# Two-block transformer on one core: pooling as running sums on GpSimd, mixers between the steps of attention, turns two steps later

## The chip, the cores and the metric

The kernel runs as one program on one core of a Trainium2 chip. Its time is the device time of one execution in microseconds (us). Before the change three runs gave 1590.38, 1590.78 and 1592.57 us; the median is 1590.78. TensorE does matmuls and transposes, VectorE (DVE), ScalarE (ACT) and GpSimd (POOL) elementwise work; each engine works through its own instructions in order and waits on semaphores. SyncE (SP) issues the loads of weights, in order too.

## The reference, cut to what matters

The model is a first block of two layers over an image stream x (256 tokens) and a context stream (256 tokens), then a second block with routed experts. All is in float32, width 1024. In each layer of the first block, three mixers read slices of one projection, and one output projection reads their results:

```python
zx = hx @ w_in[i]                      # 1280 columns: q 512, k 128, v 128, pool 256, fourier 256
mx = concatenate([
    latent_attention(q, k, v, kc, vc), # 8 heads of 64; keys: 256 context + 256 image
    pool_mix(zx[..., KV_END:POOL_END], w_pool[i], pool_scale[i]),
    fourier_mix(zx[..., POOL_END:], w_four[i]),
], axis=-1)
x = x + ga1 * (mx @ w_out[i])
if update_ctx:                         # layer 0 only: the same for the context stream
    mc = concatenate([context_attention(qc, kc, vc), pool_mix(...), fourier_mix(...)], axis=-1)

def pool_mix(u, w_pool, pool_scale):   # four groups of 64 channels, windows 2, 4, 8, 16
    means = (cs[hi] - cs[lo]) / cnt    # mean over tokens t-w/2 .. t+w/2-1, cut at the ends
    d = means - u
    return einsum('blgc,gcd->blgd', d, w_pool) * pool_scale

def fourier_mix(u, w_four):            # four groups of 64 channels
    f = fft2(u, axes=(tokens, channels), norm='ortho').real
    return einsum('blgc,gcd->blgd', f, w_four)
```

A SwiGLU follows in each layer, and then the second block, whose 32 experts of 6 MB each are the bulk of the 392 MB read from HBM.

## The kernel before, in words

Activations are held transposed: channels on partitions, tokens along the free axis, the streams side by side (512 columns in layer 0, 256 in layer 1). Each linear layer runs over tiles of 128 output channels (pe_tile, L1056 to L1074). Weights and activations are split into a high and a low part (WH, WL; HH, HL; GH, GL), and a tile is three products: high times high and high times low (L1067, L1068), then low times high (L1073). ScalarE makes the high part of a weight tile (act_split, L1026) and VectorE the low part (dve_split, L1036).

pe_layer runs, on TensorE, the in-projection of ten tiles, attention, the mixers, the output projection (eight tiles), then SwiGLU. Between the in-projection's tiles stand small jobs (pe_in_mid, pe_in_end): head norms, rotary turns, the transposes of rows (pe_rows, L1184; copy L1190), and "fills", products with the modulation weights w_ada (pe_ada, L672), which may run anywhere before they are needed. Five of ten tiles are transposed by rows: v (row 0), two pooling and two Fourier tiles (rows 1 to 4).

Attention runs in steps. A step is 128 queries of a pair of heads, g = 0 and 1. Group (0, 1) of layer 0 has 8 steps against 512 keys ("large" below) and 8 of the context stream against 256 keys ("small"); layer 1 has 8 large ones. In step x TensorE does the scores of step x into banks 0 and 1 (pe_scores, L1391), the values of the pair of steps x-3, x-2 if x is odd (pe_values, L1448), and the turns of step x-1, which are the transposes of the probabilities (pe_turn, L1422). VectorE takes the maximum (L1396) and divides (L1409, L1411), ScalarE exponentiates (L1403) and copies the turned probabilities out (act_turned, L1430). pe_scores waits until the exponentials of the step before have read the two banks (s_ex). Results are copied to MU by VectorE (L1641), from there to GH by ScalarE (L1655), and the low part is made by VectorE (L1647).

The mixers come when attention has ended (pe_mixers). Pooling is a product with a 256 by 256 matrix per window, from the table k_pool (L1695), then with w_pool (L1712). Fourier is a product along the tokens (L1701), one along the channels (L1709, L1710) and one with w_four (L1712), with copies by ScalarE between them (L1719).

SyncE fills a ring of ten slots of 1 MB. A load is issued when its slot's former content has been used. The tables k_pool and k_mix hold a slot each until the mixers have ended (consts, load.used). After the output projection TensorE waits for the norm; the fills of GAP stand there.

## Time and profile before

| what | value |
|---|---|
| median of three runs | 1590.78 us |
| the profiled execution | 1592.6 us, its span 1590.8 us |
| TensorE busy | 1392.6 us (88% of the span) |
| VectorE, ScalarE, GpSimd busy | 709.6, 522.5, 39.2 us |
| mean granted TensorE clock | 0.941 of full speed |
| layer 0: attention, mixers | 120.94 to 175.6, 175.6 to 195.0 us |
| layer 1: attention, mixers | 682.1 to 717.8, 717.8 to 731.8 us |
| transfers | 394.51 MB, mean 248 GB/s |

A busy TensorE is not TensorE at its peak, since matmuls are pipelined and a record begins while its weights or its neighbour still run. In the chain of what ended last TensorE has 65%, transfers 23%, VectorE 5% and ScalarE 4%.

### The profile page before, as it was taken

To read this page: it belongs to the slowest core of one execution; us is meant where nothing else is said; L and a number is where in the kernel's file an instruction comes from. 1 tells how busy PE (TensorE), PEld (TensorE's weight loads), DVE (VectorE), ACT (ScalarE), POOL (GpSimd) and SP (SyncE) were. 2 spreads that over 40 slices of the span, in tenths; PEclk is the share of its full clock that TensorE was granted. 3 is DMA by queue.
4 is the path that set the end of the run, shared out by engine and by line. 5 is a ranking of instruction groups with operands and counts; after the bars stand their busy time and mean duration, and the time that the engine had idled before them with its cause. 6 is when DMAs were issued, how large, how long until landed. Compare 5 with 4: busy or idle time off the path is not lost.

```text
span 1590.8 us, 24639 instructions
## 1 busy us (share of the span) xinstructions
PE 1392.6 (88%) x10297; PEld 1043.4 (66%) x10297; DVE 709.6 (45%) x1296; ACT 522.5 (33%) x967; POOL 39.2 (2%) x40
## 2 busy tenths in 40 slices
PE   6998899999999999989999999998896676676664
PEld 3664587887878787747899998898653333333332
DVE  4336546675655444664655657576421101101101
ACT  4425524222222223554543445465320110110001
POOL 1000020000000010001000000000000000000000
PEclk9999999999999999999999999999797877887878
DMA  8983043635845343705756449245799999999996
GB/s 340 412 278 122 1 159 115 219 129 183 321 161 168 114 155 106 221 16 223 234 170 211 134 172 306 89 133 219 289 420 424 426 426 426 426 426 426 426 426 266
DMA packets 160221, 394.51 MB, mean 248 GB/s; under 512 B 11605, under 2 KB 124777, under 8 KB 126058
## 3 DMA queue, kind: packets, MB, share of 16 engines
q1 hardware_dynamic: 159530, 391.44, 65.1%
q8 instruction: 84, 1.38, 0.3%
q10 hardware_dynamic: 576, 1.44, 0.2%
q14 instruction: 31, 0.25, 0.0%
HBM read 391.80 MB, written 1.05 MB: 247 GB/s over the span
## 4 chain that ended last, share of the span: by engine, by line
PE 65%; DMA 23%; DVE 5%; ACT 4%; issue 2%; SPq 0%; DVEq 0%; ACTq 0%
DMA R<-in_w_dram 22%; PE ps L1067 15%; PE ps L1073 14%; PE ps L1068 14%; PE ps L2965 3%; PE ps L1095 2%; PE ps L1089 2%; PE ps L1090 2%; PE ps L672 2%; DMA R<-in_w_ada_dram 1%; PE ps L1448 1%; PE ps L1391 1%; PE ps L3015 1%; PE ps L3044 1%; PE ps L1701 1%
## 5 line engine op out<-in xcount | busy, mean ns | idle before, releaser
L1036 DVE TENSOR_TENSOR WL<-R,WH 128x1024 fp32r<-128x1024 f32 (+1 forms) x201 | 224.5, 1133 | 162.8 <-ACT WH L1026 162.8
L2965 PE MATMUL ps<-R,XG 128*32 128x256 f32 x2048 | 176.0, 505 | 117.9 <-DMA R<-in_w_dram 112.3
L1067 PE MATMUL ps<-HH,WH 128*128 128x256 f32 (+2 forms) x872 | 273.6, 336 | 0.3 <-ACT WH L1026 0.3
L1068 PE MATMUL ps<-HL,WH 128*128 128x256 f32 (+2 forms) x872 | 270.0, 330 | 0.0
L1026 ACT ACTIVATE WH<-R 128x1024 fp32r<-128x1024 f32 (+1 forms) x201 | 190.1, 961 | 138.8 <-PE ps L1073 109.4
L2965 PEld LDWEIGHTS ps<-R,XG 128*32 128x32 f32 x2048 | 86.8, 139 | 201.8 <-issue 186.9
L1067 PEld LDWEIGHTS ps<-HH,WH 128*128 128x128 f32 (+1 forms) x872 | 164.2, 188 | 25.1 <-issue 8.1
L1068 PEld LDWEIGHTS ps<-HL,WH 128*128 128x128 f32 (+1 forms) x872 | 164.9, 189 | 16.5
L1073 PE MATMUL ps<-HH,WL 128*128 128x256 f32 (+2 forms) x872 | 164.6, 330 | 0.0
L1067 PE MATMUL ps<-GH,WH 128*128 128x512 f32 (+1 forms) x480 | 153.9, 339 | 0.0
L1068 PE MATMUL ps<-GL,WH 128*128 128x512 f32 (+1 forms) x480 | 153.4, 339 | 0.0
L1073 PEld LDWEIGHTS ps<-HH,WL 128*128 128x128 f32 (+1 forms) x872 | 133.6, 187 | 17.9 <-issue 1.1
L3004 DVE TENSOR_TENSOR HT<-ps,SIL 128x128 f32<-128x128 f32 x32 | 9.3, 292 | 297.9 <-ACT SIL L2998 297.9
L2974 ACT ACTIVATE U<-ps 128x256 f32<-128x256 f32 x32 | 19.8, 619 | 337.8 <-PE ps L2965 337.8
L1067 PEld LDWEIGHTS ps<-GH,WH 128*128 128x128 f32 x480 | 90.3, 188 | 11.8 <-issue 0.8
L1068 PEld LDWEIGHTS ps<-GL,WH 128*128 128x128 f32 x480 | 90.2, 188 | 10.9
L1073 PE MATMUL ps<-GH,WL 128*128 128x512 f32 (+1 forms) x480 | 93.3, 340 | 0.0
L1073 PEld LDWEIGHTS ps<-GH,WL 128*128 128x128 f32 x480 | 75.6, 188 | 11.0
L1147 DVE SCALAR_TENSOR_TENSOR XT<-ps,MOD,XT 128x256 f32<-128x256 f32 x80 | 36.4, 480 | 91.0 <-PE ps L1073 90.9
L1747 ACT ACTIVATE GH<-TMP 128x512 fp32r<-128x512 f32 (+1 forms) x44 | 23.1, 525 | 138.8 <-DVE TMP L1757 138.8
L3015 PE MATMUL ps<-R,HT 128*32 128x256 f32 x1024 | 62.5, 382 | 5.9 <-DVE HT L3004 3.1
L694 DVE SCALAR_TENSOR_TENSOR R<-R,SC,R 128x2048 f32<-128x2048 f32 x28 | 65.1, 2346 | 0.0
(494 smaller groups left out, 1733.9 us busy)
## 6 DMA issues: line engine op xcount, KB each, us to landing
R<-in_w_dram SPq DMA_DIRECT2D x192, 1024.0 KB, 26.5
R<-in_w_ada_dram SPq DMA_DIRECT2D x72, 1024.0 KB, 7.8
R<-in_w_gate_up_dram SPq DMA_DIRECT2D x40, 1024.0 KB, 6.9
R<-in_w_in_dram SPq DMA_DIRECT2D x20, 1024.0 KB, 9.3
R<-in_w_down_dram SPq DMA_DIRECT2D x16, 768.0 KB, 4.4
R<-in_w_down_dram SPq DMA_DIRECT2D x16, 640.0 KB, 4.3
R<-in_w_in_dram SPq DMA_DIRECT2D x8, 512.0 KB, 7.4
R<-in_w_out_dram SPq DMA_DIRECT2D x16, 256.0 KB, 8.5
```

The source lines that it names most:

```text
L672: last = e.matmul(PS[6][32 * g:32 * g + 32, :], SC[:, k, :], R[load.slot][:, 512 * g:512 * g + 512], start=(k == 0), stop=(k == 7))
L694: e.scalar_tensor_tensor(sums[x][:, :], R[load.slot][:, :], SC[:, k, v:v + 1], sums[x][:, :], ALU.mult, ALU.add)\
L1026: last = e.activation(H, w, ACT.Copy)
L1036: last = e.tensor_tensor(L, w, H.bitcast(F32), ALU.subtract)
L1067: e.matmul(b[0:n, 0:N], H[:, k, 0:n], xh(k, N), start=(k == 0), stop=False)
L1068: e.matmul(b[0:n, 0:N], H[:, k, 0:n], xl(k, N), start=False, stop=False)
L1073: last = e.matmul(b[0:n, 0:N], L[:, k, 0:n], xh(k, N), start=False, stop=(k == K - 1))
L1089: e.matmul(b[:, 0:N], room[t0 + j][0][:, k, :], xh(k, N), start=(k == 0), stop=False)
L1090: e.matmul(b[:, 0:N], room[t0 + j][0][:, k, :], xl(k, N), start=False, stop=False)
L1147: e.scalar_tensor_tensor(XT[:, j, sl], bank_of(t)[:, sl], MOD[:, i, gate + j, col:col + 1], XT[:, j, sl], ALU.mult, ALU.add).then_inc(s_xr, 1)
L2965: mm = e.matmul(PS[4][32 * g:32 * g + 32, 0:256], x[:, 4 * hf + k, :], w[g // 2][:, k, 256 * (g % 2):256 * (g % 2) + 256], start=(hf == 0 ...
L3015: mm = e.matmul(PS[6][32 * g:32 * g + 32, 0:256], HT[b % 2][:, 2 * hf + k, :], w[:, k, 256 * g:256 * g + 256], start=(hf == 0 and k == 0), ...
```

## The change

Pooling no longer uses a matrix. The in-projection's pooling tiles are copied into ZP, with 8 zero columns around each stream, and GpSimd adds shifted copies of them: windows of 2, 4, 8 and 16 come from one another, then a product with 1/count and a subtraction, 12 operations for both tiles (pool_windows). TensorE keeps the product with w_pool. For Fourier, the channel matrices are first multiplied with w_four (pe_four_weights, copied to FW), the tiles are multiplied by FW instead of transposed (pe_four_rows, copied to ZF), and one product along the tokens is left. k_pool goes.

The mixers stand between attention's steps: MIX_AT gives for a layer the step x at which one is issued, "p" pooling (tile), "f" Fourier (stream, tile), in bank 7. Scores alternate between banks 0, 1 and 5, 6; there are six probability buffers instead of four; turns are those of step x-2, values come one step later. ScalarE and VectorE make GH and GL from PSUM directly (act_high, dve_low), without MU. Both first output tiles are split during attention, and pe_out_first runs seven of eight blocks of each around the last values. Two fills go from layer 0's attention to the gap after its output projection, two from layer 1's attention into its in-projection.

```diff
-K_POOL, K_DFT, K_R1, K_D, K_RD, K_CD, K_SD = 0, 0, 1024, 1152, 1408, 1664, 1792
+K_DFT, K_R1, K_IC, K_CD, K_SD = 0, 1024, 1152, 1664, 1792
 K_END = 1920
+WINDOWS = (2, 4, 8, 16)
...
+        (oH + 18 * KB, oH + 20 * KB, oH + 22 * KB, oH + 8 * KB, oH + 10 * KB, oH + 12 * KB))]
...
-        consts.append((const_load("k_pool", 2048), const_load("k_mix", K_END)))
+        consts.append(const_load("k_mix", K_END))
...
-        plan_ada(2)
-        for load in consts[i]:
-            load.used = (s_mx, 30 if i else 20)
+        if i:
+            plan_ada(2)
+        consts[i].used = (s_mx, MIXED[i])
...
-                    plan_ada(4 if i else 6)
+                    plan_ada(4 if i else 8)
...
+    def pe_out_first(e, i, xh, xl, ready):
+        t, early, late = first_of["out", i], (4, 5, 0, 1, 6, 2, 7), (3,)
+        pe_begin(e, t)
+        pe_high(e, t, xh, xl, early, ready)
+        pe_values(e, *pair_at(i, len(STEPS[i]) + 2))
+        pe_begin(e, t + 1)
+        pe_high(e, t + 1, xh, xl, early, None)
+        for j in range(2):
+            pe_high(e, t + j, xh, xl, late, ready, begins=False)
+            pe_low(e, t + j, xh, 8)
...
+    def pe_four_weights(e, i):
+        kc = R[consts[i].slot]
+        e.wait_ge(d_ring[consts[i].slot], consts[i].landed)
+        e.wait_ge(d_wp, 128 * (i + 1))
+        e.wait_ge(s_z, i + 1)
+        e.wait_ge(s_mod, 7 if i else 2)
+        for j in range(2):
+            for x, c in enumerate((K_CD, K_SD)):
+                last = e.matmul(PS[7][:, 256 * j + 128 * x:256 * j + 128 * x + 128], kc[:, c:c + 128], WPF[:, 2 + j, :], start=True,
+                                stop=True)
+        last.then_inc(s_fm, 1)
...
+    def pe_four_rows(e, i, j, r):
+        n = round_at(i, j, r)
+        e.wait_ge(s_evi, 10 * i + 9 + j)
+        e.wait_ge(s_zf, n)
+        if (j, r) == (1, 0):
+            e.wait_ge(s_mod, TURNS.index(MORE_TURNS[i]) + 1)
+        for a in range(2):
+            c = 128 * (2 * r + a)
+            last = e.matmul(PS[7][:, 256 * a:256 * a + 256], ZT[1 + j][:, c:c + 128], FW[:, j, :], start=True, stop=True)
+        last.then_inc(s_fm, 1)
+    def dve_four_rows(e, i, j, r):
+        n = round_at(i, j, r)
+        e.wait_ge(s_fm, n + 1)
+        e.tensor_copy(ZF[:, 2 * r:2 * r + 2, j, :], PS[7][:, :].rearrange("p (a n) -> p a n", a=2)).then_inc(s_zf, 1)
...
+    WINDOW_OPS = 12
+    def pool_windows(e, i):
+        n = STREAMS_IN[i]
...
+        e.wait_ge(s_mm, first_of["in", i] + 4)
...
+        e.wait_ge(d_ring[consts[i].slot], consts[i].landed)
+        e.wait_ge(s_pads, PADS[i])
+        e.wait_ge(s_evi, 10 * i + 7)
+        e.tensor_tensor(A[:, 1:W], x0[:, 0:W - 1], x0[:, 1:W], ALU.add).then_inc(s_pm, 1)
+        e.wait_ge(s_pm, done + 1)
+        e.tensor_tensor(B[hi, 2:W - 1], A[hi, 1:W - 2], A[hi, 3:W], ALU.add).then_inc(s_pm, 1)
...
+        e.wait_ge(s_evi, 10 * i + 8)
+        e.tensor_tensor(B[:, 1:W], x1[:, 0:W - 1], x1[:, 1:W], ALU.add).then_inc(s_pm, 1)
+        e.wait_ge(s_pm, done + 6)
+        e.tensor_tensor(A[:, 2:W - 1], B[:, 1:W - 2], B[:, 3:W], ALU.add).then_inc(s_pm, 1)
...
+        e.wait_ge(s_pm, done + 11)
+        e.tensor_tensor(streams_in(x1, n), streams_in(B, n), streams_in(x1, n), ALU.subtract).then_inc(s_pm, 1)
...
-        return () if i else FILLS.get(j, ())
+        return {8: (38,), 9: (39,)}.get(j, ()) if i else FILLS.get(j, ())
...
+    def score_bank(v, g):
+        return PS[(0, 1, 5, 6)[2 * (v // 2 % 2) + g]]
...
-        if s or A == 1:
-            e.wait_ge(s_ex, 16 * A + 2 * s)
-        else:
+        if x >= 2:
+            e.wait_ge(s_ex, v - 2)
+        elif x == 0:
             e.wait_ge(*bank_out(i, 0))
             e.wait_ge(*bank_out(i, 1))
+        else:
+            e.wait_ge(s_rope, 15 * i + 15)
+            e.wait_ge(s_at, TURNS.index(MORE_TURNS[i]) + 1)
...
+        if v >= 6:
+            e.wait_ge(s_tn, v - 5)
+        e.activation(P1[v % 6][:, 0:n], score_bank(v, g)[:, 0:n], ACT.Exp, bias=stats(v)[:, 0:1], accum_out=stats(v)[:, 1:2])\
+            .then_inc(s_ex, 1)
...
-    def fills_at(A, s):
-        return {(0, 1): (24,), (0, 3): (25,), (2, 0): (38,), (2, 1): (39,)}.get((A, s), ())
...
+    MIX_AT = [{5: ("p", 0), 7: ("p", 1), 9: ("f", 0, 0), 11: ("f", 1, 0), 13: ("f", 0, 1), 14: ("f", 1, 1)},
+              {3: ("p", 0), 5: ("p", 1), 7: ("f", 0, 0), 8: ("f", 0, 1)}]
...
+        t = x - 3
+        if t < 1 or t % 2 == 0 or t >= len(STEPS[i]):
             return None
-        A, s = steps[x - 2]
+        A, s = STEPS[i][t]
...
+    def pe_mix(e, i, op):
+        kc, o = R[consts[i].slot], MIX[i].index(op)
+        if o == 0:
+            e.wait_ge(s_zf, FIRST_COPY[i] + 1 + len(ROUNDS[i]))
+        else:
+            e.wait_ge(s_gl, mix_out(i, MIX[i][o - 1]) + 1)
+        if op[0] == "p":
+            j = op[1]
+            e.wait_ge(s_pm, WINDOW_OPS * i + (5, 12)[j])
+            for s in range(STREAMS_IN[i]):
+                last = e.matmul(PS[7][:, 256 * s:256 * s + 256], WPF[:, j, :], ZP[j][:, 264 * s + 8:264 * s + 264], start=True, stop=True)
+        else:
+            _, s, j = op
+            for t in range(2):
+                for x in range(2):
+                    c = K_DFT + 512 * t + 256 * x
+                    last = e.matmul(PS[7][:, 0:256], ZF[:, 2 * s + t, j, 128 * x:128 * x + 128], kc[:, c:c + 256],
+                                    start=(t == 0 and x == 0), stop=(t == 1 and x == 1))
+        last.then_inc(s_mx, 1)
...
+    def act_high(e, op):
+        o, (m, cols) = OUTS.index(op), out_place(op)
+        if op[1] == "pair":
+            e.wait_ge(s_pv, 8 * op[2] + 2 * op[3] + 2)
+        else:
+            e.wait_ge(s_mx, mixed_by(op))
+        if op[1] == "p":
+            e.activation(GH[:, m, cols], out_bank(op), ACT.Copy, scale=out_scale(op)).then_inc(s_gh, 1)
+        else:
+            e.activation(GH[:, m, cols], out_bank(op), ACT.Copy).then_inc(s_gh, 1)
...
+    def dve_low(e, op):
+        o, (m, cols) = OUTS.index(op), out_place(op)
+        e.wait_ge(s_gh, o + 1)
+        high = GH[:, m, cols].bitcast(F32)
+        if op[1] == "p":
+            e.scalar_tensor_tensor(GL[:, m, cols], out_bank(op), out_scale(op), high, ALU.mult, ALU.subtract).then_inc(s_gl, 1)
+        else:
+            e.tensor_tensor(GL[:, m, cols], out_bank(op), high, ALU.subtract).then_inc(s_gl, 1)
...
+    def pe_attention(e, i):
+        steps = STEPS[i]
+        n = len(steps)
+        for x in range(n + 2):
+            if x < n:
                 pe_scores(e, *steps[x])
+            if x == 0:
+                pe_ada_turn(e, MORE_TURNS[i])
+            for j, r in four_round_at(i, x):
+                pe_four_rows(e, i, j, r)
+            if pair_at(i, x):
+                pe_values(e, *pair_at(i, x))
+            if x in MIX_AT[i]:
+                pe_mix(e, i, MIX_AT[i][x])
+            if x >= 2:
+                pe_turn(e, *steps[x - 2])
+    SPLIT_AT = ((12, 13), (7, 9))
+    def act_attention(e, i):
+        steps = STEPS[i]
+        n = len(steps)
+        for x in range(n + 4):
+            for op in outs_at(i, x - 1):
+                act_high(e, op)
             for g in range(2):
+                if x < n:
                     act_exp(e, *steps[x], g)
             for g in range(2):
+                if 2 <= x < n + 2:
+                    act_turned(e, *steps[x - 2], g)
+            if x in SPLIT_AT[i]:
+                act_split(e, first_of["out", i] + SPLIT_AT[i].index(x))
+    def dve_attention(e, i):
+        steps = STEPS[i]
+        n = len(steps)
+        for x in range(n + 4):
+            for g in range(2):
+                if x < n:
+                    dve_max(e, *steps[x], g)
+            if x == 0:
+                dve_ada(e, MORE_TURNS[i])
+            for j, r in four_round_at(i, x):
+                dve_four_rows(e, i, j, r)
+            if 1 <= x <= n:
                 for g in range(2):
+                    dve_divide(e, *steps[x - 1], g)
+            for op in outs_at(i, x - 1):
+                dve_low(e, op)
+            if x - 1 in SPLIT_AT[i]:
+                dve_split(e, first_of["out", i] + SPLIT_AT[i].index(x - 1))
...
-    GAP = {1: tuple(range(26, 32)), 2: tuple(range(32, 38)), 3: tuple(range(40, 44)), 4: tuple(range(44, 48))}
+    GAP = {1: tuple(range(24, 32)), 2: tuple(range(32, 38)), 3: tuple(range(40, 44)), 4: tuple(range(44, 48))}
...
-        pe_attention(e, (2,) if i else (0, 1))
-        pe_mixers(e, i)
+        pe_attention(e, i)
+        pe_out_first(e, i, gh, gl, waiting(e, mixed(i)))
...
+            pool_windows(e, 0)
             pool_sum_columns(e)
             pool_sums(e, 1, 512)
             pool_sums(e, 2, 512)
+            pool_windows(e, 1)
...
```

TensorE, step 11 of layer 0 (small), before: KTr,QT are scores, RES,P turns, PT,Z values; numbers behind names are buffers.

```order
L1391 MATMUL ps<-KTr,QT 128x256 [waits s_ex]
L1391 MATMUL ps<-KTr,QT 128x256
L1448 MATMUL ps<-PT_115,Z 64x256 [waits s_ot,s_z,s_pt]
L1448 MATMUL ps<-PT_116,Z 64x256
L1448 MATMUL ps<-PT_115,Z 64x256
L1448 MATMUL ps<-PT_116,Z 64x256
L1422 MATMUL ps<-RES,P_110 128x128 [waits s_pt,s_nrm]
L1422 MATMUL ps<-RES,P_110 128x128
L1422 MATMUL ps<-RES,P_111 128x128 [waits s_pt,s_nrm]
L1422 MATMUL ps<-RES,P_111 128x128
```

The same engine in the changed kernel, from the scores of step 11 (R,ZF is the Fourier mix):

```order
L1517 MATMUL ps<-KTr,QT 128x256 [waits s_ex]
L1517 MATMUL ps<-KTr,QT 128x256
L1636 MATMUL ps<-R_63,ZF 128x256 [waits s_gl]
L1636 MATMUL ps<-R_63,ZF 128x256 x3
L1549 MATMUL ps<-RES,P_113 128x128 [waits s_pt,s_nrm]
L1549 MATMUL ps<-RES,P_113 128x128
L1549 MATMUL ps<-RES,P_114 128x128 [waits s_pt,s_nrm]
L1549 MATMUL ps<-RES,P_114 128x128
L1517 MATMUL ps<-KTr,QT 128x256 [waits s_ex]
L1517 MATMUL ps<-KTr,QT 128x256
L1572 MATMUL ps<-PT_119,Z 64x256 [waits s_gl,s_z,s_pt]
L1572 MATMUL ps<-PT_120,Z 64x256
```

A mix stands between the scores and the turns, the turned probabilities are those of two steps before, and the mix waits on s_gl, VectorE's low part of the mix before it.

VectorE, step 5 of layer 0, before (ps is PSUM, P the probabilities):

```order
L1396 TENSOR_REDUCE ST<-ps 128x1 [waits s_sco] x2
L1641 COPY MU_108<-ps 128x256 [waits s_pv]
L1409 RECIPROCAL ST<-ST 128x1 [waits s_ex]
L1411 TENSOR_SCALAR P_112<-P_112,ST 128x512 [waits s_rcp]
L1409 RECIPROCAL ST<-ST 128x1 [waits s_ex]
L1411 TENSOR_SCALAR P_113<-P_113,ST 128x512 [waits s_rcp]
```

VectorE in the changed kernel, the same step (L1663 is the low part of values, straight from PSUM):

```order
L1522 TENSOR_REDUCE ST<-ps 128x1 [waits s_sco] x2
L1536 RECIPROCAL ST<-ST 128x1 [waits s_ex]
L1538 TENSOR_SCALAR P_115<-P_115,ST 128x512 [waits s_rcp]
L1536 RECIPROCAL ST<-ST 128x1 [waits s_ex]
L1538 TENSOR_SCALAR P_116<-P_116,ST 128x512 [waits s_rcp]
L1663 TENSOR_TENSOR GL<-ps,GH 128x256 [waits s_gh]
```

The divides (P) are now those of the step before the maximum's, and the copy to MU is gone.

GpSimd in the changed kernel, layer 0's running sums for the second pooling tile; before, this engine had nothing there:

```order
L1294 TENSOR_TENSOR ZS_76<-ZP_74 128x535 [waits s_evi]
L1296 TENSOR_TENSOR ZS_75<-ZS_76 128x533 [waits s_pm]
L1298 TENSOR_TENSOR ZS_76<-ZS_75 128x529 [waits s_pm]
L1300 TENSOR_TENSOR ZS_75<-ZS_76 64x521 [waits s_pm]
L1301 TENSOR_TENSOR ZS_76<-ZS_76,R_63 64x2x256
L1303 TENSOR_TENSOR ZS_76<-ZS_75,R_63 64x2x256 [waits s_pm]
L1305 TENSOR_TENSOR ZP_74<-ZS_76,ZP_74 128x2x256 [waits s_pm]
```

Each waits for the one before it (s_pm); the first waits for ScalarE's copy of the tile (s_evi).

## Rows read from the trace of the kernel before

**Rows 1.** The page's 40 slices: share of the transfer engines in tenths.

```profile
DMA  8983043635845343705756449245799999999996
```

**Rows 2.** Stretches: us, busy PE PEld DVE ACT POOL, clock, transfers.

```profile
121.00:153.30 32.30, 25.99 (x159) 13.18 (x158) 21.98 (x54) 18.90 (x48) 0.00 (x0) 0.95 0.42 139
153.30:175.60 22.30, 17.72 (x122) 9.77 (x124) 16.84 (x60) 16.10 (x57) 0.00 (x0) 1.00 0.01 1
175.60:195.00 19.40, 18.71 (x81) 11.08 (x79) 7.48 (x16) 9.09 (x21) 0.00 (x0) 1.00 0.00 1
682.10:717.80 35.70, 29.05 (x184) 15.09 (x185) 22.72 (x56) 21.34 (x52) 0.00 (x0) 0.95 0.00 0
717.80:731.80 14.00, 10.35 (x43) 5.39 (x40) 4.73 (x10) 5.34 (x11) 0.00 (x0) 1.00 0.01 1
```

**Rows 3.** Timeline, large steps: start us, us, engine, line, what, [idle before].

```profile
141.89 1.13 PE L1391 MATMUL ps<-KTr,QT 64*128 64x512 f32 x4 [1.42 <-ACT P L1403]
...
145.85 1.13 PE L1391 MATMUL ps<-KTr,QT 64*128 64x512 f32 x4
...
147.01 1.29 DVE L1396 TENSOR_REDUCE ST<-ps 128x1 f32<-128x512 f32 x2 [0.43 <-PE ps L1391]
147.74 0.69 ACT L1403 ACTIVATE P<-ps,ST 128x512 f32<-128x512 f32 x1 [0.83 <-DVE ST L1396]
...
149.08 1.08 ACT L1430 ACTIVATE PT<-ps 128x512 f32<-128x512 f32 x2
...
149.24 1.13 PE L1391 MATMUL ps<-KTr,QT 64*128 64x512 f32 x4 [1.23 <-ACT P L1403]
...
150.30 1.95 PE L1448 MATMUL ps<-PT,Z 128*64 128x256 f32 x16
...
152.18 1.09 PE L1422 MATMUL ps<-RES,P 128*128 128x128 f32 x8
```

**Rows 4.** Chain of waits, small steps: start us, us, what.

```profile
161.24 0.70 PE ps L1391 x4
161.95 1.06 PE ps L1448 x8
...
165.82 0.70 PE ps L1391 x4
```

**Rows 5.** Chain of waits, layer 1's mixers.

```profile
725.19 0.45 PE ps L1710 x2
...
726.86 1.73 PE ps L1701 x4
```

**Rows 6.** Timeline of the gap after layer 0's output projection.

```profile
243.70 4.50 PE L672 MATMUL ps<-R,SC 128*32 128x512 f32 x40
...
247.18 0.89 DVE L926 SCALAR_TENSOR_TENSOR HL<-TMP,MOD,HH 128x256 fp32r<-128x256 f32 x2 [0.18 <-ACT HH L876]
```

**Rows 7.** GpSimd's additions by line: shortest, median, longest in ns.

```profile
L818 POOL TENSOR_TENSOR TMP<-TMP,TMP x20: 737/1301/2207, 208.0 to 945.9; 128x512 f32<-128x512 f32 x10, 128x256 f32<-128x256 f32 x10
```

**Rows 8.** Timeline: GpSimd's additions and VectorE's splits beside them.

```profile
207.85 1.22 DVE L1036 TENSOR_TENSOR WL<-R,WH 128x1024 fp32r<-128x1024 f32 x1
208.02 2.20 POOL L818 TENSOR_TENSOR TMP<-TMP,TMP 128x512 f32<-128x512 f32 x1 [12.47 <-DVE TMP L805]
...
213.55 1.30 POOL L818 TENSOR_TENSOR TMP<-TMP,TMP 128x512 f32<-128x512 f32 x1 [3.33 <-ACT TMP L798]
214.46 1.47 DVE L1036 TENSOR_TENSOR WL<-R,WH 128x1024 fp32r<-128x1024 f32 x1 [1.65 <-ACT WH L1026]
```

**Rows 9.** The page's loads: what, issuer, KB, median us to landing.

```profile
R<-in_w_gate_up_dram SPq DMA_DIRECT2D x40, 1024.0 KB, 6.9
```

**Rows 10.** Timeline of SyncE from the first expert load.

```profile
1053.28 141.72 SPq L2611 DMA_DIRECT2D R<-in_w_dram  x48
```

**Rows 11.** Timeline, end of the in-projections of layer 0 and layer 1.

```profile
108.49 1.99 PE L1270 MATMUL ps<-QT,R 128*128 128x256 f32 x8 [1.44 <-DVE QT L1257]
...
681.13 0.42 DVE L1190 COPY Z<-ps 128x256 f32<-128x256 f32 x1
```

More of the change, by code:

```diff
@@ L553, in block_program @@
         j = t - first_of["in2"]
-        tile.bank = t % 4 if j < 0 else j if j < 4 else (j - 4) % 3 if j < N_IN2 else (j - N_IN2) % 4
+        out = next((t - first_of["out", i] for i in range(2) if 0 <= t - first_of["out", i] < 8), None)
+        tile.bank = out % 4 if out is not None else t % 4 if j < 0 else j if j < 4 else (j - 4) % 3 if j < N_IN2 else (j - N_IN2) % 4
         tile.after = last_in.get(tile.bank)
@@ L1051, in block_program, with pe_begin @@
     bank_free = {}
-    def pe_tile(e, t, xh, xl, ready, mid=None):
-        tile, b = tiles[t], bank_of(t)
-        n, N = tile.n, tile.N
-        H, L = room[t][0:2]
-        K = sum(p[2] for p in tile.parts)
+    def pe_begin(e, t):
+        tile = tiles[t]
         if t in bank_free:
@@ L1482, in act_attention, with outs_at, attention_out, mix_out @@
-    def act_attention(e, group):
-        steps = steps_of(group)
-        for x in range(len(steps) + 2):
+    def outs_at(i, x):
+        mix, pair = MIX_AT[i].get(x), pair_at(i, x)
+        return ([(i, *mix)] if mix else []) + ([(i, "pair", *pair)] if pair else [])
+    OUTS_OF = [[op for x in range(len(STEPS[i]) + 3) for op in outs_at(i, x)] for i in range(2)]
+    OUTS = OUTS_OF[0] + OUTS_OF[1]
+    def attention_out(A, m):
+        return OUTS.index((A_LAYER[A], "pair", A, m))
+    def mix_out(i, op):
+        return OUTS.index((i, *op))
@@ L1660, in block_program @@
[L1660 to L1672 removed]
     for i in range(2):
+        end = (32, 48)[i]
         for j in range(4):
[L1676 to L1678 removed]
@@ L1714, in act_mixers @@
[L1714 to L1733 removed]
+            bank_free[first_of["out", i] + j] = (s_ex, end - 2) if j < 2 else (s_pt, end)
@@ L1875, in act_layer @@
         t1 = first_of["gu", i, 0]
-        act_linear(e, first_of["out", i], 8, sums(2 * i + 1, ("out", i)), begun=1, then=t1)
+        act_linear(e, first_of["out", i], 8, sums(2 * i + 1, ("out", i)), begun=2, then=t1)
         act_split(e, t1 + 1)
```

392 lines of the change are left out of this document (160 added, 232 removed).

## The prediction

> **What bounds the kernel now.** I read the page's 40 slices first: the DMA row says that only the last quarter of the span is bound by transfers [rows 1]. That tail can't start by itself: its loads go out from 1053 us on, when ring slots come free behind the second block's compute [rows 10], so a microsecond saved in the first block moves the whole tail forward by one. Then I read the stretches around the change [rows 2]. In layer 0 attention takes 32.3 + 22.3 us (image queries against 512 keys, then context queries against 256) and the mixers after it 19.4 us, until the output projection starts: 74.0 us. In layer 1 it is 35.7 + 14.0 = 49.7 us. In none is TensorE full: 26.0 of 32.3, 17.7 of 22.3, 29.1 of 35.7. In the mixers' stretches VectorE and ScalarE idle more than half the time.
>
> Last, the pace of attention, step by step. Two large steps take 7.35 us (scores at 141.89 and at 149.24) [rows 3], two small ones 4.58 us (161.24, 165.82) [rows 4]. What sets 7.35: scores to their first reduce 1.16, to the first exponential 0.73, two exponentials 1.34, two copies of turned probabilities 1.08, hand-over 0.1, and on TensorE values 1.88 and turns 1.02.
>
> **Does attention itself get faster?** It has one more pair of score banks, six probability buffers and turns two steps late, so scores no longer wait for the exponentials of the step just before. But ScalarE's order in a step is exponentials of step x, then the turned copies of step x-2, and the values of a pair, on TensorE in the step after, wait for those copies. Call S the moment at which TensorE starts the scores of an odd step. The exponentials are done at S + 1.16 + 0.73 + 1.34 = 3.23, the copies of the second half of the pair at 4.31, values start at 4.4, end at 6.3, turns follow to 7.3, and only then come the next odd scores. That is 7.3 us for two steps [rows 3], as now. So I give attention no faster pace. What the order buys is the hole between S + 3 (scores, turns, next scores issued) and S + 4.4: a mixer's matmuls fit there.
>
> **Layer 0, summed from the first scores to the output projection.**
> - Start, to the scores of step 5: first scores, a turn of the ada block, two Fourier rounds whose copies (0.7 each, near a reduce of that width, 1.29 for two) are queued on VectorE ahead of the first two divides, no overlap yet: 15.4 us by following the queue with the durations of [rows 3].
> - Steps 5 to 8, two pairs, with both pooling mixes (two matmuls of 256 columns, 0.45 each [rows 5]) in the hole: 2 x 7.3 = 14.6.
> - Steps 9 and 10 are small, with a Fourier mix of four 256-column matmuls, priced as the two of 512 columns now, 1.73 [rows 5]. TensorE sets it: 0.7 scores + 1.73 + 1.02 turns of a large step + 0.65 for their copy on ScalarE + 0.1, then the last large values 1.88 and small turns 0.5: 6.6.
> - Steps 11 and 12: 0.7 + 1.73 + 0.5 + 0.7, values 1.06 [rows 4], turns 0.5: 5.2.
> - Steps 13 and 14 hold a mix each in one bank. The second waits for VectorE's low half of the first, and VectorE has the first output tile's split (1.22, as the split in [rows 8]) and the maxima and divides of two steps ahead of it. Behind it on TensorE wait the turns of step 12 and the scores of step 15: 8.9 for the pair.
> - Steps 15 to 17, draining: 5.0. Then the projection begins, with the last values (1.06) inside: seven of eight blocks of tile 0 cover the copy that they wait for.
> Sum 15.4 + 14.6 + 6.6 + 5.2 + 8.9 + 5.0 + 1.1 = 56.8 against 74.0: 17.2 less. This pays for itself mostly by the mixers' 19.4 us lying beside attention.
>
> **Layer 1.** Same start but one Fourier round: 14.6 to step 5; steps 5 and 6 7.3; from step 7 with a Fourier mix in steps 7 and 8, the second waiting for the low half of the first: values end at 6.4, low half at 6.4, mix to 8.2, turns of step 6 to 9.2, their copy, turns of step 7 to 10.4; last values in the projection 1.9. Sum 34.2 against 49.7: 15.5 less.
>
> **In-projection, both layers.** Four row transposes with copies go; a product of the Fourier matrices (four matmuls of 128 columns, one copy) and two rounds (one in layer 1) come. In layer 0 a copy ahead of the last head products goes, where TensorE idles 1.44 us [rows 11], but TensorE gets about 0.7 more afterwards: +0.4. In layer 1 the last row copy before the scores goes (681.13 [rows 11]), and two ada fills of 0.9 come in; TensorE has that much idle there: +0.3.
>
> **Fills moved.** Two ada fills leave layer 0's attention for the gap after the output projection. The gap is full: five fills take 4.50 us from 243.70, the first low half of the norm starts at 247.18, so it is there at about 248.1, just as they end [rows 6]. Two more at 0.9: +1.8, all on the path, since afterwards TensorE is the bound.
>
> **GpSimd's running sums.** 12 tensor operations a layer; one of 512 columns takes 1.30 us, of 256 0.74 [rows 7]. So 17 us in layer 0 from about 96 us, 9 in layer 1 from about 666; the first is wanted some 35 us later, the last some 25. Hidden. But they run beside the rotary additions and the weight splits on VectorE. Those rows [rows 8] show what happens then: an addition on GpSimd that began 0.17 us behind a split took 2.20 instead of 1.30, and a split that began while one ran took 1.47 instead of 1.22. Each waits for the other to end. In layer 0 VectorE has about 4 us to spare before the last Fourier round, so I charge 1.0; in layer 1, with half the length, 0.7. The ends are 0 (all in gaps) and 8 x 1.3 - 4 = 6.4 with 8 x 0.74 = 5.9. The Trainium skill (SBUF, "Who interferes with whom") calls this an exclusive lock between GpSimd and a VectorE instruction with two SBUF inputs, the second to issue blocked in full; by that rule, the trace agrees, the upper ends are the price. The Trainium skill (Perfetto Trace Analysis, "Per-engine timelines") also warns that a GpSimd span in a profile is unreliable; if so only the 17 us above moves.
>
> **DMA.** 2 MB of pooling tables go. The ring has a slot more, but the ada loads of the gap now sit behind the slot of the mixing table, free only after the last mix, and SwiGLU's second gate load gets the slot of the first, free when VectorE has split the third SwiGLU tile. TensorE then has the low parts of four tiles ahead of the tile that needs it, 7 to 8 us by my estimate, and such a load lands in 6.9 [rows 9] with a split of 1.0 behind it. I charge 0, at worst 3.
>
> **Sum.** -17.2 - 15.5 + 0.4 + 0.3 + 1.8 + 1.0 + 0.7 = -28.5. The profiled execution took 1592.6 us for a span of 1590.8; the median of the runs is 1590.78. 1592.6 - 28.5 = 1564.1, and on the median's scale 1562.3. I say 1562.5.
>
> **Rivals.**
> - *Attention gets faster too.* If each engine ran at its own work, a pair of large steps would take TensorE 2 x 1.13 + 1.88 + 2 x 1.02 = 6.2, not 7.3; over eight such pairs -9: 1553.5. For: the change aims its order at it, and VectorE and ScalarE would be just under 6.2. Against: the chain through ScalarE above.
> - *The lock bites.* The rotary additions wait for GpSimd every time: upper ends, 6.4 + 5.9 in place of 1.7, +10.6: 1573. For: [rows 8]. Against: GpSimd pauses between dependent operations, and in layer 1 the sums end about when the additions start.
> - *The mixers aren't hidden.* Their matmuls, 1.8 + 6.9 in layer 0 and 0.9 + 3.5 in layer 1, each lengthen their step, and so do Fourier rounds and their copies: of 28.5, 13.1 are lost, with 3 for the late gate load: 1578.5.
> - *Slower: running sums late.* TensorE's queue is in order; at step 7 (layer 0) and step 5 (layer 1) it waits for the twelfth sum with scores, values and turns queued behind. Seven sums have 38 us in layer 0 and 28 in layer 1. With c for a long operation the waits are 7c - 38 and 3.5c - 28; they eat the 28.5 at c = 9.0 us. At c = 10, 32 + 7 = 39: 1601. Against: 1.30, and 2.21 blocked. For: the trace has neither 64-partition nor broadcast operands on GpSimd.
>
> **How the numbers follow.** Forecast 0.62 (its own range 1556 to 1570: a microsecond either way for each of its waits), faster attention 0.13, the lock 0.11, mixers not hidden 0.11, slower 0.03. The range 1553 to 1577 takes the first three and the edge of the fourth. A difference of 0.2%, 3.2 us, is about what can be told from none. Faster 0.96, same 0.01, slower 0.03.
>
> **What would show it.** Right: large steps still about 7.3 us a pair; output projections starting some 57 and 34 us after the first scores; no stretch of mixers; TensorE waiting in step 14 for VectorE; GpSimd ending before 125 and before 685 us less what was saved; the same tail, earlier. Wrong: pairs near 6.2, rotary additions that wait for GpSimd, a TensorE wait for GpSimd, a wait for the gate load at the first SwiGLU tiles.

## The result

The changed kernel took 1566.2 us, the median of four runs (1563.99 to 1567.12); the kernel before 1591.67, the median of four as well. The ratio is 0.984, with a 95% interval of 0.9825 to 0.9855: 25.5 us less, where 28.5 were forecast. In a second session it ran in 1563.8 against 1591.5, 27.7 less. The kernel before ran once more beside every group of experiments below; its medians there are 1591.4 to 1591.8, so the groups can be compared. The profiled execution took 1567.12 us, its span 1565.3, against 1592.6 and 1590.8.

The page of the changed kernel: each engine's busy time, and the transfer row that answers to [rows 1].

```profile
PE 1378.6 (88%) x10253; PEld 1042.5 (67%) x10253; DVE 699.1 (45%) x1270; ACT 512.5 (33%) x947; POOL 65.5 (4%) x74
...
DMA  8990326545853532815764368337799999999995
```

TensorE is busy 14 us less. The tail is bound by transfers as before and starts earlier. These are the two attentions, mixers inside, answering to [rows 2] (us, busy PE PEld DVE ACT POOL, clock, transfers).

```profile
120.30:177.00 56.70, 50.59 (x302) 31.03 (x302) 40.77 (x115) 38.49 (x110) 0.34 (x4) 0.97 0.12 45
668.10:700.20 32.10, 28.99 (x175) 17.13 (x173) 22.90 (x57) 22.24 (x56) 0.00 (x0) 1.00 0.03 7
```

Where the time went, read from the start of the first instruction of each stretch, with the sum's terms beside it:

| stretch | before | after | difference | forecast |
|---|---|---|---|---|
| to layer 0's first scores | 120.94 | 120.25 | -0.7 | +1.4 |
| layer 0, scores to output projection | 73.85 | 56.49 | -17.4 | -18.3 |
| layer 0, projection and gap to the first gate matmul | 53.52 | 56.85 | +3.3 | +2.9 |
| layer 0, SwiGLU's first four tiles (late gate load) | 22.35 | 22.82 | +0.5 | 0 |
| the rest of SwiGLU | 361.99 | 362.09 | +0.1 | 0 |
| layer 1, in-projection | 49.38 | 49.55 | +0.2 | +1.0 |
| layer 1, scores to output projection | 49.31 | 32.15 | -17.2 | -17.4 |
| layer 1, projection and gap | 30.96 | 34.09 | +3.1 | +1.9 |
| layer 1, SwiGLU | 197.19 | 197.20 | 0 | 0 |
| second block, to the first expert load | 93.79 | 95.07 | +1.3 | 0 |
| from there to the end | 537.52 | 538.74 | +1.2 | 0 |

To the end of layer 1 the forecast -28.5 met -28.0. Then 2.5 came back in code that the change doesn't touch.

The large steps, which answer to [rows 3] (chain of waits of the changed kernel: start, us, what; L1517 scores, L1630 pooling mix, L1549 turns, L1557 turned copies, L1572 values, L1529 exponentials):

```profile
139.48 1.95 PE ps L1572 x16
141.43 1.02 PE ps L1549 x8
142.46 1.06 PE ps L1517 x4
143.51 1.06 PE ps L1630 x4
144.58 0.89 PE ps L1549 x8
...
145.52 0.20 ACT P L1529
145.72 0.98 ACT PT L1557 x2
...
146.75 1.95 PE ps L1572 x16
```

Values start every 7.27 us, and ahead of them stands ScalarE's pair of copies behind its last exponential. The mix takes 1.06 and lengthens nothing: it stands in the hole. In the run with all mixers behind attention (below) the same two steps, now without a mix, take 7.26 as well.

The end of layer 0's attention (chain, as above; L1039 is VectorE's split, L1663 a low part, L1636 a Fourier mix, L1071 the output projection):

```profile
164.31 1.13 DVE WL L1039
165.45 0.67 DVE ST L1522 x2
...
167.03 0.34 DVE GL L1663
...
167.42 1.99 PE ps L1636 x8
169.41 0.44 PE ps L1549 x4
169.85 0.68 PE ps L1517 x4
170.53 0.74 DVE ST L1522 x2
...
172.18 0.68 DVE GL L1663 x2
...
172.99 1.97 PE ps L1572 x8
```

The mix of step 14 waits for VectorE, as forecast. What follows wasn't seen: two low parts of step 14 are made together, behind the maxima of step 15, and the next values wait for them. Something else wasn't seen either: these values take 1.97 for eight matmuls, where the pair of steps before took 1.08. The timeline and windows of this stretch (the clock third from the right) say why:

```profile
165.20 1.08 PE L1572 MATMUL ps<-PT,Z 128*64 128x256 f32 x8
...
172.99 1.97 PE L1572 MATMUL ps<-PT,Z 128*64 128x256 f32 x8 [1.93 <-DVE GL L1663]
```

```profile
169.80:172.90 3.10, 1.27 (x9) 0.70 (x8) 2.32 (x9) 2.65 (x10) 0.08 (x3) 1.00 0.78 246
172.90:176.30 3.40, 3.17 (x13) 1.74 (x14) 0.79 (x4) 0.64 (x2) 0.00 (x0) 0.50 1.02 426
```

TensorE was busy 1.27 of 3.10 us, and then its granted clock was 0.50. The repeat of this kernel and the run with the third output tile split ahead show the same at this place.

Layer 1's third output tile, from the timeline (idle before and its releaser at the end):

```profile
709.20 0.36 PE L1071 MATMUL ps<-GH,WH 128*128 128x256 f32 x1 [0.94 <-ACT WH L1029]
```

### The profile page after: what moved, and what is told of

It reads as the page before. It is cut to its first block, busy times and chain, and to the rows that moved or that the text cites. A ratio compares the mean times of both kernels' runs of the same rounds, so it can differ in the third digit from the quotient of the medians.

```text
span 1565.3 us, 24504 instructions
## 1 busy us (share of the span) xinstructions
PE 1378.6 (88%) x10253; PEld 1042.5 (67%) x10253; DVE 699.1 (45%) x1270; ACT 512.5 (33%) x947; POOL 65.5 (4%) x74
## 3 DMA queue, kind: packets, MB, share of 16 engines
q10 hardware_dynamic: 576, 1.44, 0.2%
## 4 chain that ended last, share of the span: by engine, by line
PE 62%; DMA 24%; DVE 6%; ACT 5%; issue 2%; SPq 0%; DVEq 0%; ACTq 0%
DMA R<-in_w_dram 22%; PE ps L1071 15%; PE ps L1072 15%; PE ps L1079 15%; PE ps L3073 3%; PE ps L1122 2%; DMA R<-in_w_ada_dram 1%; PE ps L1116 1%; PE ps L1572 1%; PE ps L670 1%; PE ps L1117 1%; PE ps L1549 1%; DVE HL L929 1%; PE ps L1517 1%; ACT WH L1029 1%
## 5 line engine op out<-in xcount | busy, mean ns | idle before, releaser
L1039 DVE TENSOR_TENSOR WL<-R,WH 128x1024 fp32r<-128x1024 f32 (+1 forms) x201 | 225.2, 1137 | 165.1 <-ACT WH L1029 165.1
L1071 PE MATMUL ps<-HH,WH 128*128 128x256 f32 (+2 forms) x872 | 273.5, 335 | 0.3 <-ACT TMP L1851 0.3
L1071 PEld LDWEIGHTS ps<-HH,WH 128*128 128x128 f32 (+1 forms) x872 | 164.3, 188 | 26.2 <-issue 8.6
L1072 PEld LDWEIGHTS ps<-HL,WH 128*128 128x128 f32 (+1 forms) x872 | 164.9, 189 | 16.4
L1071 PE MATMUL ps<-GH,WH 128*128 128x512 f32 (+1 forms) x480 | 154.2, 340 | 1.3 <-ACT WH L1029 1.3
L1071 PEld LDWEIGHTS ps<-GH,WH 128*128 128x128 f32 x480 | 90.3, 188 | 14.2 <-issue 3.5
```

Of the source, the lines that this page charges most:

```text
L1039: last = e.tensor_tensor(L, w, H.bitcast(F32), ALU.subtract)
L1071: e.matmul(b[0:n, 0:N], H[:, k, 0:n], xh(k, N), start=(begins and k == ks[0]), stop=False)
L1072: e.matmul(b[0:n, 0:N], H[:, k, 0:n], xl(k, N), start=False, stop=False)
```

## The experiments

Times below are medians; "layer 0" and "layer 1" are the stretches from first scores to output projection, 56.4 and 32.2 us in the changed kernel. Those stretches repeat within 0.2 us between profiles of the same attention code, the time of a whole run within 2 or so.

**The changed kernel again.**

> The changed kernel once more, as the yardstick for the others on the same chip. 1566.2 us. Its profile is also read for two places behind the first block where the first profile gave back 2.5 us of the 28.0 that were saved by 746 us: 1.3 between the second block's start and its first expert load, where TensorE's granted clock fell to half for longer (8.3 us against 4.5), and 1.2 in the tail. If both are chance, this profile differs there by as much in either direction; if the change causes them, they stand here again within 0.3 us.

1563.8 us (1562.74 to 1564.32). Layers 56.39 and 32.15. The second block took 95.31 to its first expert load, the tail 535.1. Over all thirteen profiles of the changed kernel and its variants the former is 93.7 in two and 95.1 to 95.4 in eleven, before it was 93.8; the tail runs from 534.6 to 538.9, before it was 537.5. So the tail is chance. The 1.3 has two values, and they go with the clock: in the eleven TensorE's clock was at half for 6.8 us of that stretch in all, in the two and in the kernel before for 3.4. Why more variants meet the longer one isn't shown. Here is where it lies in the changed kernel's first profile (columns as above, the clock third from the right):

```profile
970.20:985.70 15.50, 13.10 (x89) 12.44 (x88) 9.88 (x26) 5.04 (x16) 0.00 (x0) 0.78 0.37 113
```

**All mixers behind attention.**

```diff
-    MIX_AT = [{5: ("p", 0), 7: ("p", 1), 9: ("f", 0, 0), 11: ("f", 1, 0), 13: ("f", 0, 1), 14: ("f", 1, 1)},
-              {3: ("p", 0), 5: ("p", 1), 7: ("f", 0, 0), 8: ("f", 0, 1)}]
+    MIX_AT = [{19: ("p", 0), 20: ("p", 1), 21: ("f", 0, 0), 22: ("f", 1, 0), 23: ("f", 0, 1), 24: ("f", 1, 1)},
+              {11: ("p", 0), 12: ("p", 1), 13: ("f", 0, 0), 14: ("f", 0, 1)}]
```

> The mixers in their new form, but all after attention's last step, one behind the other. My theory (overlap pays): a pooling mix then costs 0.9 + 0.7 + 0.7 + 0.2 = 2.5 us in layer 0, 1.5 in layer 1, a Fourier mix 1.73 + 0.4 + 0.42 + 0.2 = 2.75; together 16.0 and 8.5. Back come what they add to the steps now, some 7.5 in layer 0 (steps 9 to 14 and the drain) and 2.4 in layer 1; the last values lose their cover, about 1 a layer. Net +16.5: 1583 us. Rival (the new form pays, and each mix lengthens its step by its own time): only the copies between mixes come on top, +5: 1571 us.

The loops of the three engines are lengthened to match, and the last values move from the output projection back behind the last turns.

1590.91 us: 27.1 more, the whole gain gone (ratio to the kernel before 0.9997, 0.9983 to 1.0011). Layers 74.77 and 42.65. The new form by itself, in this serial order, is worth nothing; the overlap is worth more than the 16.5 I expected. Part of the excess stands in this kernel's timeline and windows; I didn't account for the rest:

```profile
179.06 3.78 PE L1635 MATMUL ps<-R,ZF 128*128 128x256 f32 x8 [1.56 <-DVE GL L1660]
183.77 3.78 PE L1635 MATMUL ps<-R,ZF 128*128 128x256 f32 x8 [0.93 <-DVE GL L1662]
```

```profile
173.70:178.90 5.20, 2.23 (x10) 1.32 (x8) 1.82 (x3) 1.76 (x3) 0.00 (x0) 0.93 0.01 3
178.90:192.00 13.10, 11.08 (x24) 7.57 (x24) 0.95 (x3) 0.77 (x2) 0.00 (x0) 0.51 0.00 0
```

Three of layer 0's four Fourier mixes take twice their 1.9 us, at a granted clock of 0.51, which is the 1.2 GHz level, after a stretch in which TensorE was busy 2.23 of 5.20 us.

**The same, with TensorE kept busy.** One product into an unused bank behind each mix.

```diff
                 pe_mix(e, i, MIX_AT[i][x])
+                e.matmul(PS[5][:, 0:512], ident, RES[:, 0:512], start=True, stop=True)
```

> As the run with all mixers behind attention, plus one product of 512 columns into an unused bank behind each mix, so that TensorE doesn't stand still while ScalarE and VectorE make the halves; the product is thrown away. In that run three of four Fourier mixes of layer 0 took 3.8 us in place of 1.9, in a stretch with a granted clock of 0.51 of full speed, entered after TensorE had been busy 2.2 of 5.2 us. My theory (the half clock follows from TensorE's idling between the mixes, and is 5.7 us of that run's 27): the mixes take 1.9 to 2.0 again, layer 0 from first scores to projection falls from 74.8 to 69 to 70, layer 1 stays at 42.7 or gains up to half a microsecond a mix in waiting for the extra product: 1585 us against 1590.9. Rival (the half clock has to do with something else than idling): the mixes stay at 3.8, and the extra products cost up to a microsecond each on top: 1592 or more.

1586.61 us, 4.3 less than without the extra products. Layer 0 71.43 (3.3 less), layer 1 43.11 (0.5 more).

```profile
180.76 1.99 PE L1635 MATMUL ps<-R,ZF 128*128 128x256 f32 x8 [0.70 <-DVE GL L1660]
182.60 1.02 PE L1681 MATMUL ps<-RES 128*128 128x512 f32 x2
183.69 1.99 PE L1635 MATMUL ps<-R,ZF 128*128 128x256 f32 x8
```

```profile
180.00:193.00 13.00, 12.07 (x45) 8.09 (x45) 2.41 (x5) 1.54 (x4) 0.34 (x4) 1.00 0.07 10
```

More work, less time: with the gaps filled the mixes run at full clock, so the half clock there came from TensorE's idling between them. This rests on one profile of each kernel; the ten runs without the extra products spread from 1585.55 to 1593.45, for a reason not traced, the seven with them from 1584.42 to 1588.05. The Trainium skill (TensorE: Matmul & The Clock Gate, "Part 1: The HAM clock gate (the 'warmup' mystery)") says that the throttled clock is the default and activity releases it; these two runs agree. The layer came out 1.4 to 2.4 longer than expected because the last values and the first pooling mix (1.97 and 1.94, for 1.08 and 1.06) still ran at half clock.

**Turns one step later instead of two.**

```diff
-        t = x - 3
+        t = x - 2
...
-                pe_turn(e, *steps[x - 2])
+                pe_turn(e, *steps[x - 1])
...
-                    act_turned(e, *steps[x - 2], g)
+                    act_turned(e, *steps[x - 1], g)
```

> Turns are those of step x-1 again, values a step earlier; mixers stay at their steps. My theory (turns two steps later brings no pace, only a hole at the right place): a large pair without a mix is still 7.3, but the hole now lies ahead of the values and the mix stands behind them, so each mix adds its own time: 0.9 twice in layer 0, about 1.1 for each Fourier mix there, 0.45 twice and about 1.9 in layer 1. About +6: 1572 us, large pairs with a pooling mix 8.2 in layer 0. Rival (turns two steps later gives the pace): pairs over 7.5 without a mix too, +10 or more: 1577. Rival (it brings nothing): 1566.

1588.36 us, 24.6 more; layers 66.39 and 45.01. All three expectations missed. The chain of this kernel (L1538 is the divide):

```profile
136.00 1.11 PE ps L1517 x4
137.11 1.27 DVE ST L1522 x2
...
138.49 0.50 DVE P L1538
...
139.03 1.25 PE ps L1549 x8
```

VectorE divides the probabilities of a step behind the next step's maxima, an order made for late turns. Early turns then wait for the scores issued just ahead of them: 4.3 us a step. So the run undid half a change. (The cut leaves out two loop ends that follow from it.)

**The same, with VectorE's order undone too.**

```diff
-            if 1 <= x <= n:
+            if x < n:
                 for g in range(2):
-                    dve_divide(e, *steps[x - 1], g)
+                    dve_divide(e, *steps[x], g)
```

> As the run with turns of step x-1, which took 24.6 us more than the changed kernel, but VectorE divides the probabilities of step x right behind its maxima, as the kernel before does. In that run the turns of x-1 waited for a divide that VectorE had queued behind the maxima of step x, and so for the scores of x: 4.3 us a step. My theory (that queue was the loss, and turns two steps later by itself gives only the place of the hole): +6 on 1563.8: 1570 us; large pairs without a mix 7.3. Rival (turns two steps later is the pace itself, whatever VectorE's order): 1580 or more, pairs over 8.

1580.21 us, 16.4 more; layers 65.50 and 37.71. The first large pair, without a mix, took 7.44 (values at 130.32 and 137.76), so the pace without mixes is nearly the same, as I held. The second such pair, now with a pooling mix, took 9.0, not the 8.2 of the expectation before:

```profile
137.76 1.95 PE ps L1572 x16
139.70 1.06 PE ps L1630 x4
140.76 0.87 PE ps L1549 x8
141.64 1.11 PE ps L1517 x4
142.75 0.68 DVE ST L1522
...
145.13 0.49 DVE P L1538
145.62 0.66 DVE GL L1661
146.28 0.34 DVE GL L1663
...
146.76 1.95 PE ps L1572 x16
```

The mix stands behind the values and not in the hole, and the next values wait for low parts that VectorE has queued behind divides, which wait for exponentials. TensorE waits more, and its clock is low in places here too: values 3.17 in place of 1.95 at 154.81, a mix 3.15 at 178.59. Between my +6 and the rival's "1580 or more" the time sides with the rival, the pair without a mix with me. The mixers' places weren't tried anew for this order, so 16.4 is the price of it with the mixers where they were.

**Turned copies ahead of the exponentials on ScalarE.** In act_attention the loop over act_turned moves above the loop over act_exp.

> ScalarE copies the turned probabilities of step x-2 before the exponentials of step x, not behind them. My theory (the pace of large steps is the chain scores, maximum, exponentials, turned copies, values): values no longer wait for the exponentials, and a large pair falls from 7.27 us to TensorE's own work, 2 x 1.06 + 1.95 + 2 x 1.02 = 6.1 plus the mix in it (0.9 in layer 0, 0.45 in layer 1): 7.0 and 6.6. Over two such pairs and the start in layer 0 and three in layer 1 about -4: 1562 us, small steps unchanged. Rival (ScalarE then waits for turns, its exponentials come later, and the next scores and divides with them): no change or slower, 1566 to 1570 us, pairs 7.3 or more.

1561.76 us; layers 54.85 and 31.82, so -1.9 where -4 was expected. A pair fell from 7.27 to 7.01 in both layers: as said in layer 0, but 6.6 was expected in layer 1. Layer 1 lost its gain again in step 8, whose mix waited for the low part of the one before: ScalarE had the output tile's split (step 7) ahead of its high part.

**Layer 0's mixers earlier.**

```diff
-    MIX_AT = [{5: ("p", 0), 7: ("p", 1), 9: ("f", 0, 0), 11: ("f", 1, 0), 13: ("f", 0, 1), 14: ("f", 1, 1)},
+    MIX_AT = [{3: ("p", 0), 5: ("p", 1), 7: ("f", 0, 0), 9: ("f", 1, 0), 11: ("f", 0, 1), 13: ("f", 1, 1)},
```

> Layer 0's mixers at steps 3, 5, 7, 9, 11, 13 in place of 5, 7, 9, 11, 13, 14; nothing else. The changed kernel ran in 1563.8 us beside these, with 56.4 from the first scores to the output projection. My theory (the drain is long because the mix of step 14 waits 1.1 us for VectorE, and ScalarE's copy of the values of that step stands behind the turned copy that this mix holds up): steps 13 and 14 fall from 8.2 to 5.3, steps 15 to 17 from 7.1 to 5.0; the Fourier mix that now stands in a large step (1.92 against a hole of 1.1 to 1.4) and the earlier pooling mix give back about 1.5. 52.9, 1560.3 us. Rival (TensorE has its own work to do wherever the mix stands, and the drain is long for lack of anything to overlap): 56.0 to 56.8, 1564.

1561.55 us; layer 0 53.08, expected 52.9. The sum is met and its terms only in part. Steps 13 and 14 fell from 8.2 to 5.2, as said: the mix of step 14 had made them long. But the drain, steps 15 to 17, fell only from 7.0 to 6.2, not to 5.0. TensorE waits there even longer ahead of the values, now behind VectorE's second split and the maxima after it (1.13 and 0.34 us in the chain), while the values themselves run at full clock:

```profile
171.59 1.08 PE L1572 MATMUL ps<-PT,Z 128*64 128x256 f32 x8 [2.21 <-ACT PT L1557]
```

The granted clock of the whole drain is 1.00 here, 0.50 for 3.4 us of it in the changed kernel. So the drain's gain is the clock's, not the copies'. What decides whether the clock falls after such a wait isn't shown: it fell after 1.93 us of it and not after these 2.21.

**The third output tile split ahead.**

```diff
+            if j == 0 and begun == 2:
+                ahead = 2
             while done < min(ahead + 1, n):
```

> ScalarE and VectorE split the third tile of each output projection before, not behind, the square and the residual of the first. My theory: the waits of 0.4 us (layer 0) and 0.94 (layer 1) before that tile's first matmul go, -1.4: 1562.4 us; the stretch from the first output matmul to the first gate matmul falls from 56.9 to 56.4 in layer 0 and from 34.1 to 33.1 in layer 1. Rival (the split waits anyway for the first tile's low part, which ends 1.2 us before the second tile's in layer 1, and a split with its hand-over takes 1.2): no change in layer 1, 0.4 in layer 0: 1563.4.

1564.15 us, within the spread of the changed kernel. The stretches show it: 56.85 to 56.22 and 34.09 to 33.72. In layer 0 the wait is gone whole. In layer 1 the wait of 0.94 is gone too (the tile starts at 708.16, as the one before it ends), but that tile and the next two now take 3.16, 3.11 and 3.14 us in place of 2.88: half of the gain goes to three short delays.

**Three edits at once.** Copies first, splits ahead, mixers at 3, 5, 7, 9, 11, 13 and 2, 3, 5, 7.

> Three edits at once: turned copies before the exponentials, mixers earlier in both layers (3, 5, 7, 9, 11, 13 and 2, 3, 5, 7), the third output tile split ahead. With turned copies first alone attention took 54.9 and 31.8 us, and in layer 1 the mix of step 8 waited for the low part of the one before, behind a split. My theory: layer 0 to 50.5 (the waits of steps 13, 14 and the drain gone, TensorE at its own work in large steps), layer 1 to 30.3, 1.4 less in the projections: 1563.8 - 9 = 1555 us. Rival (with TensorE at its own work the earlier mixers only lengthen large steps): 54 and 31.5, 1560.

1562.8 us; layers 53.54 and 33.21: in time nearly the rival's number, but not for its reason. Large steps were at TensorE's pace to 152 us, and the loss came behind: VectorE's two splits stood in the chain, the values of the drain waited 2.61 us, and the clock then was at half for 6.8 us (granted 0.50 from 168.70 to 175.50), so that the drain took 8.1. In layer 1 two mixes one step apart cost a wait of 3.44 us.

**Splits at 15 and 17, layer 1's mixers at 2, 4, 6, 8**, and beside it the same with the exponentials first.

> The three edits of before (turned copies first, layer 0's mixers at 3, 5, 7, 9, 11, 13, third tile split ahead) with two things mended that cost them their gain: layer 1's mixers at 2, 4, 6, 8, never one step behind the other, so that none waits for the low part of the one before; and the splits of layer 0's first two output tiles by ScalarE and VectorE at steps 15 and 17 instead of 12 and 13, where VectorE's 1.13 us stood in the chain twice. My theory: layer 0 falls from 53.5 to 51.5, layer 1 from 33.2 to 31.0, with 1.0 less in the projections 7 less than the changed kernel: 1557 us. Rival (a split belongs in the chain wherever it stands, since the projection waits for it): 53.5 or more in layer 0 and only layer 1's gain: 1560.

> The same as the run beside it (mixers at 3, 5, 7, 9, 11, 13 and 2, 4, 6, 8, splits at 15 and 17, third tile ahead), but with the exponentials ahead of the turned copies again. My theory (the order of ScalarE sets the pace of large steps): large pairs 7.3 in place of 7.0, layer 0 52.5, layer 1 31.8; 1.5 to 2 more than the run beside it: 1559 us. Rival (with the mixers spread evenly, TensorE is at its own work in either order): the same as beside it within 0.5.

1559.18 and 1562.46 us. Layer 0 came to 50.93 and 52.20: within 0.6 of my theory. Only the second compares cleanly with the run with layer 0's mixers earlier, 53.08, since both have the exponentials first and full clock: moving the splits took the drain from 6.2 to 5.3. The 2.6 between three edits at once and the first of these two is splits and clock together. ScalarE's order is worth 1.3. Layer 1 missed: 34.60 and 36.30. In even steps a mix stands together with values, and the holes of the odd steps stay empty. The clock fell there, on this row of the first of the two:

```profile
688.20 3.62 PE L1574 MATMUL ps<-PT,Z 128*64 128x256 f32 x16 [2.29 <-DVE GL L1665]
```

**The best of it.** Layer 1 back at 3, 5, 7, 8.

```diff
-    SPLIT_AT = ((12, 13), (7, 9))
+    SPLIT_AT = ((15, 17), (8, 9))
```

> Layer 0 as in the run with even steps (50.9 us), layer 1's mixers back at the odd steps 3, 5, 7 and at 8, where they were best (at 2, 4, 6, 8 they stood behind the values and attention took 34.6 with turned copies first, in place of 31.8), and the split of layer 1's first output tile at step 8, not 7. My theory: with turned copies first and the split at 7 the mix of step 8 waited some 1.3 us for the high and low part of the one before, which ScalarE made behind the split; so layer 1 falls to 30.5, and the kernel to 1555 us. Rival (the split's 1.05 us only moves to another place of ScalarE's queue and holds up the last turned copies): layer 1 31.8 and 1556.5.

1557.69 us (1555.53 to 1560.28, five runs; ratio to the kernel before 0.9789, 0.9776 to 0.9803), some 6 less than the changed kernel. Layers 50.83 and 31.71, both at full clock:

```profile
120.20:171.00 50.80, 48.65 (x300) 30.36 (x300) 39.78 (x113) 36.58 (x108) 0.34 (x4) 1.00 0.14 53
661.30:693.00 31.70, 29.04 (x177) 17.51 (x173) 21.53 (x55) 21.75 (x54) 0.00 (x0) 1.00 0.05 15
```

In layer 0 TensorE is now busy 48.65 of 50.80. Layer 1 sides with the rival: the mix of step 8 waits wherever the split stands. From the mix before it to this one 5.9 us pass, 6.6 with copies first and the split at step 7, 5.5 in the changed kernel; with the split moved it waits for divides behind the exponentials.

## Why the prediction held, and where it didn't

- *No faster pace in attention.* Held: 7.27 a pair. Copies first showed the chain to be the one named, and also that little lies behind it (0.3 a pair), since a mix then takes the room.
- *Layer 0's attention.* 55.7 forecast without the last values, 56.5 measured. Steps 5 to 12: 14.5, 6.7, 5.2 against 14.6, 6.6, 5.2. The start took 14.9 for 15.4, steps 13 and 14 8.2 for 8.9; that these errors and the next partly cancel is luck. The step that failed is "Steps 15 to 17, draining: 5.0": it was 7.0. I gave TensorE its full clock there, and it ran at half for 3.4 us. From start to start the values took 1.91 for 1.02 and what follows to the projection 1.84 for 1.44 in the run with the mixers earlier: 1.3 of the 2.0, by an estimate from these rows. I also followed TensorE out of step 14 but not ScalarE and VectorE, whose copies of that step's values stood behind those of the late mix: 0.3, the second low part in the chain. The term was small even without both: at full clock, with mixers and splits out of its way, the drain takes 5.3.
- *Layer 1's attention.* 32.3 forecast, 32.15 measured. Not all of that gain is overlap. The kernel before had 3.4 us at half clock in this stretch (the 0.95 in [rows 2]), the changed one has none:

```profile
700.62 1.61 PE L1391 MATMUL ps<-KTr,QT 64*128 64x512 f32 x4 [1.43 <-ACT P L1403]
702.16 3.10 PE L1448 MATMUL ps<-PT,Z 128*64 128x256 f32 x16
```

 Against 1.13 and 1.95 in [rows 3] some 1.6 us of the 17.2 are the clock's, by an estimate from these rows. My sum had every step at full clock without saying so, and here that came true. Layer 0 of the kernel before had such a stretch too, from 124.3; the changed kernel has one in its drain instead.
- *"This pays for itself mostly by the mixers' 19.4 us lying beside attention".* Held: with the mixers behind attention layer 0 is 18.4 longer and layer 1 10.5; the last values now lie in these stretches and no longer in the projections, so it is 27.1 in the time. Of these 4.3 were regained by extra products that kept the clock.
- *In-projection and lock.* Forecast +1.4 and +1.0, measured -0.7 and +0.2. The idle 1.44 ahead of layer 0's head products [rows 11] vanished whole:

```profile
107.01 1.89 PE L1384 MATMUL ps<-QT,R 128*128 128x256 f32 x8
```

 The first scores also vary by chance (119.9 to 121.6 over kernels with the same code up to there). Two of twelve sums in layer 0 were blocked, 2.16 and 2.17 in place of 1.1 to 1.3, and the sums of a tile ended 37 us or more before its mix:

```profile
98.19 1.07 POOL L1296 TENSOR_TENSOR ZS<-ZS 128x533 f32<-128x533 f32 x1
99.34 1.07 POOL L1298 TENSOR_TENSOR ZS<-ZS 128x529 f32<-128x529 f32 x1
100.49 2.17 POOL L1300 TENSOR_TENSOR ZS<-ZS 64x521 f32<-64x521 f32 x1
```

 In layer 1 two of twelve took 1.41 and 1.72 in place of 0.6 to 0.85, with 20 us to spare. The waiting is real [rows 8] and cost nothing that these stretches can show. It wasn't tried by itself.
- *Fills moved, +1.8.* The gap from the last output matmul grew by 1.5.
- *Gate load, 0, at worst 3.* 0.5: it left at 247.12, landed 6.2 later, and the tile that needs it began at 256.41 instead of 255.94.
- *Projections.* The mis-sized term: only the values inside were counted. Starting both first tiles early leaves the third tile's split with no lead: it waits 0.40 and 0.94, and in all the projection loses 0.6 and 1.2 by it.
- *"The same tail, earlier".* 2.5 came back behind the first block, 1.2 of it chance, 1.3 a longer half clock stretch in the second block, which most but not all variants have.

The rivals: faster attention needed pairs of 6.2 and even the reordered kernel reaches 7.0; the lock cost nothing visible; no sum was late. That the mixers aren't hidden has a part of the truth. The pooling mixes are hidden whole, but layer 0's four Fourier mixes, 7.7 us of matmuls, make steps 9 to 14 5.0 longer than in the run with all mixers behind attention (6.70, 5.23 and 8.20 against 5.71, 4.49 and 4.88). With the mixers earlier steps 7 to 14 are 2.4 longer.
